# Two-block transformer on one core: values multiplied step by step, latent heads in pairs, side steps one slab later, weight chunks 528 bytes apart

## The reference, cut to what matters

```python
x = first_block(x, c, ctx, c_ctx, ...)    # layer 0: dense GQA + pool mixer; layer 1: window GQA with sink
x = second_block(x, norm_mix_2, ...)      # layer 0: dsa_mixer + diff_mixer; layer 1: nsa_mixer
```

```python
q_lat = einsum('bthd,hdc->bthc', q_nope, w_uk)                 # (T, 8, 128)
s = q_lat . c_kv  +  q_rope . k_rope                           # widths 128 and 32
p = softmax(where(chosen, s * A_SCALE, -inf));  o_lat = p @ c_kv
```

## Time and profile before

| | |
|---|---|
| time, median of 3 runs | 3372.45 us (3364.27 to 3375.6) |
| the profiled execution's own time | 3378.23 us |
| its span | 3376.4 us |
| TensorE busy | 3076.1 us (91%) |
| VectorE, ScalarE, GpSimd busy | 1709.3, 1101.2, 1052.0 us |
| granted TensorE clock, mean | 0.943 |
| matmul records | 16970 |
| HBM read | 253.03 MB, 76 GB/s |

### The profile page before, as it was taken

One profiled execution on the slowest core, in us unless ns is written; L12 is line 12 of the kernel. 1 busy time (PEld: TensorE's weight loads), 2 busy tenths in 40 slices (PEclk: granted clock), 3 DMA queues, 4 the chain that ended last, 5 costly groups with the idle time before them and its releaser, 6 DMA issues.

```text
span 3376.4 us, 48629 instructions
## 1 busy us (share of the span) xinstructions
PE 3076.1 (91%) x16970; PEld 2493.5 (74%) x16970; DVE 1709.3 (51%) x2892; ACT 1101.2 (33%) x1904; POOL 1052.0 (31%) x573
## 2 busy tenths in 40 slices
PE   6778779999997888899998999899999999899997
PEld 3666668888886766699895765688887866688886
DVE  4755768864335566433245766342333247643433
ACT  3145143111124255432224324352223226552222
POOL 1121122323322311244443420244444301244443
PEclk8889989999998899899999988899999969999998
DMA  6200413434211100222222210222223100022222
GB/s 238 77 1 8 142 63 127 171 124 137 75 50 45 43 1 33 67 89 93 94 84 69 75 38 1 80 98 93 93 93 118 55 15 2 14 97 96 93 94 81
DMA packets 74344, 258.83 MB, mean 77 GB/s; under 512 B 9456, under 2 KB 12016, under 8 KB 72688
## 3 DMA queue, kind: packets, MB, share of 16 engines
q1 hardware_dynamic: 60256, 205.61, 18.4%
q10 hardware_dynamic: 13968, 51.65, 4.5%
HBM read 253.03 MB, written 2.10 MB: 76 GB/s over the span
## 4 chain that ended last, share of the span: by engine, by line
PE 81%; DVE 6%; issue 6%; ACT 3%; DVEq 1%; SPq 1%; ACTq 1%; POOL 0%; DMA 0%; POOLq 0%; PEldq 0%
PE ps L822 56%; PE ps L800 6%; PE ps L2513 2%; PE ps L2499 2%; PE ps L2656 1%; PE ps L426 1%; PE ps L1862 1%; PE ps L1095 1%; DVE ps L389 1%; PE ps L2720 1%; PE ps L1666 1%; DVE nm L1711 1%; ACT w_hi L638 1%; PE ps L2633 1%; PE ps L2632 1%
## 5 line engine op out<-in xcount | busy, mean ns | idle before, releaser
L760 POOL TENSOR_TENSOR w_lo<-w_raw,w_hi 128x1024 fp32r<-128x1024 f32 (+1 forms) x373 | 919.6, 2468 | 1823.5 <-ACT w_hi L638 1823.5
L638 ACT ACTIVATE w_hi<-w_raw 128x1024 fp32r<-128x1024 f32 (+1 forms) x373 | 385.6, 1038 | 1192.3 <-PE ps L822 948.0
L822 PE MATMUL ps<-h_hi,w_hi 128*128 128x258 f32 (+2 forms) x1824 | 315.6, 326 | 50.1 <-ACT w_hi L638 46.1
L822 PEld LDWEIGHTS ps<-h_hi,w_hi 128*128 128x128 f32 x1824 | 268.4, 195 | 85.6 <-issue 45.1
L822 PE MATMUL ps<-h_lo,w_hi 128*128 128x258 f32 (+2 forms) x1824 | 299.7, 316 | 0.0
L822 PE MATMUL ps<-h_hi,w_lo 128*128 128x258 f32 (+2 forms) x1824 | 296.7, 314 | 0.0
L822 PEld LDWEIGHTS ps<-h_lo,w_hi 128*128 128x128 f32 x1824 | 260.2, 190 | 24.4 <-DVE h_lo L2275 0.4
L822 PEld LDWEIGHTS ps<-h_hi,w_lo 128*128 128x128 f32 x1824 | 258.4, 189 | 23.1
L918 DVE CAST act_hi<-f_t 128x512 f32 (+1 forms) x88 | 165.8, 1884 | 12.6
L822 PE MATMUL ps<-hb_hi,w_hi 128*128 128x512 f32 x672 | 166.7, 390 | 2.0 <-issue 1.7
L822 PE MATMUL ps<-hb_hi,w_lo 128*128 128x512 f32 x672 | 166.0, 389 | 0.0
(11 more groups left out here) (345 smaller groups left out, 5179.9 us busy)
## 6 DMA issues: line engine op xcount, KB each, us to landing
w_raw<-in_ffn_in SPq DMA_DIRECT2D x176, 512.0 KB, 3.4
mod_row<-in_w_mod_rows ACTq DMA_DIRECT2D x80, 512.0 KB, 4.3
w_raw<-in_ffn_out SPq DMA_DIRECT2D x64, 512.0 KB, 3.4
w_raw<-in_ev_in SPq DMA_DIRECT2D x26, 512.0 KB, 3.5
w_raw<-in_ffn_out SPq DMA_DIRECT2D x32, 384.0 KB, 3.0
w_raw<-in_od_in SPq DMA_DIRECT2D x21, 512.0 KB, 3.4
mod_ring<-in_w_mod SPq DMA_DIRECT2D x8, 1024.0 KB, 13.2
w_raw<-in_wo_in SPq DMA_DIRECT2D x12, 512.0 KB, 3.5
```

Of the source, the lines that this page charges most:

```text
L638: act.activation(k.w_hi[:, s, 0:self.KT * P], k.w_raw[:, s, 0:self.KT * P], ACT.Copy).then_inc(k.sems["w_hi_ready"], 1)
L760: ins = pool.tensor_tensor(k.w_lo[:, s, 0:self.KT * P], k.w_raw[:, s, 0:self.KT * P], k.w_hi[:, s, 0:self.KT * P].bitcast(F32), ALU.subtract)
L822: ins = pe.matmul(k.ps[:, self.step * s + g, 0:t1 - t0], w[:, s, c * P:(c + 1) * P], h[:, c, t0:t1], start=(n == 0), stop=(n == len(parts) ...
```

## The change

1. `PairAttend` gets an option `spread` apart from `one`. The latent stage uses `PairAttend` without either: 4 turns of two heads by 4 query blocks. The value product of a batch takes both heads' probabilities as one moving operand of up to 512 columns. `hn_col` and `hn_rcol` move to make room.
2. `Attend` deals out the products of a batch over the Z steps in every stage, and signals `pv_ready` at i = Z - 1.
3. Side steps 0, 1 and 2 all come after slab 2.
4. In linears with a shift the chunks of `w_hi` and `w_lo` lie 528 bytes apart (`wide = P + 4`); `h_lo` moves by 128 bytes, and the bases of the buffers by multiples of 256.

```diff
+        self.wide = P + (4 if norm is not None and norm.shift is not None else 0)
...
-        act.activation(k.w_hi[:, s, 0:self.KT * P], k.w_raw[:, s, 0:self.KT * P], ACT.Copy).then_inc(k.sems["w_hi_ready"], 1)
+        act.activation(self.parts(k.w_hi, s), self.raw(s), ACT.Copy).then_inc(k.sems["w_hi_ready"], 1)
+    def parts(self, t, s):
+        return t[:, s, 0:self.KT * self.wide].rearrange("p (c w) -> p c w", w=self.wide)[:, :, 0:P]
+    def raw(self, s):
+        return self.kit.w_raw[:, s, 0:self.KT * P].rearrange("p (c w) -> p c w", w=P)
...
-                ins = pe.matmul(..., w[:, s, c * P:(c + 1) * P], h[:, c, t0:t1], ...)
+                ins = pe.matmul(..., w[:, s, c * self.wide:c * self.wide + P], h[:, c, t0:t1], ...)
...
             if self.beside:
-                self.beside.tensor(pe, m)
+                for step in (range(3) if m == 2 else [m]):
+                    self.beside.tensor(pe, step)
...
             self.two(pe, order)
-            if self.beside:
-                for m in range(2):
-                    self.beside.tensor(pe, m)
             self.slabs(pe, tile, 2)
...
-            if self.spread:
-                part = lambda i: len(products) if i else 0
-            else:
-                part = lambda i: len(products) * i // self.Z // 2 * 2 if i < self.Z else len(products)
+            part = lambda i: len(products) * i // self.Z // 2 * 2 if i < self.Z else len(products)
...
-            if i == (0 if self.spread else self.Z - 1):
+            if i == self.Z - 1:
                 ins.then_inc(S["pv_ready"], 1)
...
-            if self.one:
+            if not self.spread:
                 pe.wait_ge(*self.count("prepared", p + 1))
-                if p >= 2:
-                    pe.wait_ge(*self.count("pt_b", p - 1))
+            if self.one and p >= 2:
+                pe.wait_ge(*self.count("pt_b", p - 1))
...
-    k.h_lo = at("h_lo", [P, DC, TOK + 4], F32R, H + 24704)
+    k.h_lo = at("h_lo", [P, DC, TOK + 4], F32R, H + 24832)
-    k.w_hi = at("w_hi", [P, 2, KMAX * P], F32R, W + 8192)
-    k.w_lo = at("w_lo", [P, 2, KMAX * P], F32R, W + 16384)
+    k.w_hi = at("w_hi", [P, 2, KMAX * P + 64], F32R, W + 8192)
+    k.w_lo = at("w_lo", [P, 2, KMAX * P + 64], F32R, W + 16896)
...
+    turns2 = [(j, half) for j in range(2) for half in range(2)]
+    def scores_latent(pe, s, turn, qi):
+        j, half = turns2[turn]
+        n, q = (qi + 1) * P, slice(qi * P, (qi + 1) * P)
+        for a in range(2):
+            pe.matmul(s[:, a, :], k.qlat[:, 4 * j + 2 * half + a, q], k.ckv_s[:, 0:n], start=True, stop=False, skip_group_check=True)
+        for a in range(2):
+            at = 32 * (2 * half + a)
+            rows = slice(at, at + 32)
+            pe.matmul(s[:, a, :], k.qkv2[rows, 12 + j, q], k.qkv2[rows, 1, 0:n], start=False, stop=False, skip_group_check=True, tile_position=(at, 0))
+        for a in range(2):
+            ins = pe.matmul(s[:, a, :], k.ident_b, k.chosen[:, qi, 0:n], start=False, stop=True, skip_group_check=True)
+        return ins
+    def scaled(dve, chain, rinv, probs, turn, qi):
+        return dve.tensor_tensor(probs, probs, rinv.unsqueeze(2).to_broadcast([P, 2, (qi + 1) * P]), ALU.mult)
+    def latent_pv(pe, o, b):
+        both = o.rearrange("p (a q) -> p a q", a=2)
+        for i, (slot, t, c0, c1) in enumerate(causal_terms(b % 2)):
+            ins = pe.matmul(both[:, :, c0:c1], k.ckv_tok[:, t, :], k.pt_pair[:, b % 2, :, slot, c0:c1], start=(i == 0), stop=True, skip_group_check=True)
+        return ins
+    PairAttend(k, len(turns2), scores_latent, latent_pv, scaled, latent_out, k.pt_pair)
```

More of the change, by code:

```diff
@@ L799, in two @@
             for g, (t0, t1) in enumerate(self.groups):
-                ins = pe.matmul(k.ps[:, self.step * s + g, 0:t1 - t0], w[:, s, c * P:(c + 1) * P], h[:, c, t0:t1], start=(e not in begun), stop=(left[e] == 0))
+                ins = pe.matmul(k.ps[:, self.step * s + g, 0:t1 - t0], w[:, s, c * self.wide:c * self.wide + P], h[:, c, t0:t1], start=(e not in begun), stop=(left[e] == 0))
             begun.add(e)
@@ L821, in tile @@
                 for g, (t0, t1) in enumerate(self.columns(m) if self.latent else self.groups):
-                    ins = pe.matmul(k.ps[:, self.step * s + g, 0:t1 - t0], w[:, s, c * P:(c + 1) * P], h[:, c, t0:t1],
+                    ins = pe.matmul(k.ps[:, self.step * s + g, 0:t1 - t0], w[:, s, c * self.wide:c * self.wide + P], h[:, c, t0:t1],
                                     start=(n == 0), stop=(n == len(parts) - 1))
@@ L1802, with __init__ @@
 class PairAttend(Stage):
-    def __init__(self, kit, J, scores, pv, prepare, finish, pt, one, adds=None):
+    def __init__(self, kit, J, scores, pv, prepare, finish, pt, one=False, spread=False, adds=None):
         super().__init__(kit)
+        self.spread = spread
         self.J, self.N, self.B, self.scores, self.pv, self.prepare, self.finish, self.pt, self.one, self.adds = J, J * QT, J * 2, scores, pv, prepare, finish, pt, one, adds
@@ L1816, in __init__ @@
             ("tr_a", 0 if one else self.N), ("pt_a", 0 if one else self.N), ("tr_b", self.N), ("pt_b", self.N),
-            ("pv_ready", self.B), ("spread_ready", 0 if one else self.B), ("o_free", self.B),
+            ("pv_ready", self.B), ("spread_ready", self.B if spread else 0), ("o_free", self.B),
             ("part_ready", self.B if adds else 0), ("part_used", self.B if adds else 0))}
@@ L1868, in output @@
                 pe.wait_ge(*self.count("pt_a", 2 * b + 2))
+            if self.spread:
                 pe.wait_ge(*self.count("prepared", 2 * b + 2))
@@ L1892, in take @@
         def take(b):
-            dve.wait_ge(*self.count("pv_ready" if self.one else "spread_ready", b + 1))
+            dve.wait_ge(*self.count("spread_ready" if self.spread else "pv_ready", b + 1))
             if self.adds and b >= 2:
@@ L1934, in scalar @@
                 exp(p + 1)
-            if not self.one and p >= 3 and p % 2 == 1:
+            if self.spread and p >= 3 and p % 2 == 1:
                 spread((p - 3) // 2)
@@ L1938, in scalar @@
             act.activation(self.turned(p, 0 if self.one else 1), k.ps[:, self.bank(p, 1), 0:(p % QT + 1) * P].rearrange("p (t c) -> p t c", c=P), ACT.Copy).then_inc(S["pt_b"], 1)
-        if not self.one:
+        if self.spread:
             spread(self.B - 1)
@@ L2394, in memory @@
     k.ln_eps = small("ln_eps", [P, 1])
-    k.hn_col, k.hn_rcol = small("hn_col", [P, 64]), small("hn_rcol", [P, 64])
     k.eps = small("eps", [P, 1])
@@ L2628, in plan @@
                  + [{"slab": 14 + m, "hi": k.qkv2_hi[:, 14 + m, :], "lo": k.lo_2[:, m, :]} for m in range(8)], latent_in, d["w_uk"])
-    def scores_latent(pe, s, j, a, qi):
-        rows, n, q = slice(32 * a, 32 * a + 32), (qi + 1) * P, slice(qi * P, (qi + 1) * P)
-        pe.matmul(s[:, 0:n], k.qlat[:, 4 * j + a, q], k.ckv_s[:, 0:n], start=True, stop=False, skip_group_check=True)
-        pe.matmul(s[:, 0:n], k.qkv2[rows, 12 + j, q], k.qkv2[rows, 1, 0:n], start=False, stop=False, skip_group_check=True, tile_position=(32 * a, 0))
-        return pe.matmul(s[:, 0:n], k.ident_b, k.chosen[:, qi, 0:n], start=False, stop=True, skip_group_check=True)
@@ L2636, in whole_pv @@
-    def whole_pv(v, head):
-        def pv(pe, o, j, n):
-            return [lambda i=i, slot=slot, t=t, c0=c0, c1=c1: pe.matmul(
-                o[:, c0:c1], v(j, t), k.pt4[:, n % 2, head(n), slot, c0:c1], start=(i == 0), stop=True, skip_group_check=True)
-                for i, (slot, t, c0, c1) in enumerate(causal_terms(n % 2))]
-        return pv
-    Attend(k, 2, [[(n // 2, 2 * (n % 2) + i, i, True) for i in range(2)] for n in range(8)], scores_latent,
-           causal_tiles, lambda n, qi: 0, whole_pv(lambda j, t: k.ckv_tok[:, t, :], lambda n: n // 2 % 2),
-           lambda dve, chain, j, u, a, qi, probs, rinv: dve.tensor_scalar(probs, probs, rinv, None, ALU.mult), no_marks,
-           lambda dve, chain, o, j, n: dve.tensor_copy(k.qkv2[:, 4 + 4 * j + n // 2, 256 * (n % 2):256 * (n % 2) + 256], o[:, 0:256]), k.pt4)
+    turns2 = [(j, half) for j in range(2) for half in range(2)]
@@ new lines, in scaled, with latent_out @@
+    def scaled(dve, chain, rinv, probs, turn, qi):
[5 more added lines that the diff above has]
+        return ins
+    def latent_out(dve, o, b):
+        first = 4 + 4 * turns2[b // 2][0] + 2 * turns2[b // 2][1]
+        return dve.tensor_copy(k.qkv2[:, first:first + 2, 256 * (b % 2):256 * (b % 2) + 256], o.rearrange("p (a q) -> p a q", a=2))
```

15 lines of the change are left out of this document (5 added, 10 removed).

## The result

The changed kernel takes 3344.65 us (median of 4, 3342.71 to 3347.7) against 3370.89 for the kernel before: ratio 0.9921, interval 0.9907 to 0.9935, so 22 to 31 us less. The forecast was 3357 in a range from 3335. The profiled execution took 3345.04 us, span 3343.3, which is 33.1 less than the profiled one before; that one was some 6 us above the median of its kernel, so differences between these two profiles add up to more than the medians differ by. TensorE is busy 3060.1 us of the span, 92%.

A forecast was written before the change was run, and what follows sets the result against it. TensorE was taken to set the time nearly everywhere, the linears' slabs carrying 56% of the span. Terms -7 (latent pairs), -3 (side steps), 0 (values), -5 (chunks) gave -15 us on the median 3372.45: 3357 us, range 3335 to 3377.

The forecast's parts named there:

- The sum: Whole kernel: -7 - 3 + 0 - 5 = -15 us, on the median 3357 us.
- Latent heads in pairs, -7: Latent stage: one of two rotated products and one switch per block go, one wait is added; -14 to +3 us.
- the wait for `prepared`: Latent stage: TensorE waits before the transposes for VectorE's maximum, copies and scaling, 2.0 us once a turn.
- The VectorE rival: Paired latent stage: scaling late at two blocks a turn, stage keeps 86.6 us, total 3364; chance 0.14 with another rival.
- Values dealt out, 0: Window stages -5 us, dense +3, context +2 from dealing out value products; sum 0, from -8 to +29.
- the price of a switch: Value batches: switching TensorE to two column halves and back takes 0.34 us, paid four times a batch.
- +3 and +2: Dealt-out values: dense stage 3 us longer, context stage 2 us longer.
- The rival of the switches (+29): Value batches: each portion pays 0.34 us and holes stay, +29 us, total 3386; chance 0.12.
- Side steps, -3: `wo_in`: slab 2 starts 2.9 us earlier, nothing gained in `ev_in` and `od_in`; from -4 to +1 us.
- Chunks 528 apart, -5: Shifted linears, 110 slabs: 2 ns a pair saved; bounds a gain of 21 us and a loss of 13.
- the reading of 4 ns between `ha` and `wo_out`: Single 512-column matmuls: part in step 1.98 us, part out of step 2.01, taken as 4 ns a matmul better.
- the distance does nothing: Shifted linears: weights and tokens do not meet in SBUF; weights part 0 to +13 us, total 3366; chance 0.20.

The follow-up runs named there:

- same_32_rows: The changed kernel, but both heads of a pair take their rotated product on the same 32 rows; 0.9940 of the kernel before.
- scale_first: The changed kernel, with VectorE scaling block p+1 before the maximum of block p+2 in all stages with paired heads; 0.9913 of the kernel before.
- values_alone: The kernel before with only the values dealt out over the units; 0.9960 of the kernel before.
- values_in_two: The changed kernel with values of the dense, context and window stages dealt out in two portions a batch instead of four; 0.9961 of the kernel before.
- the second: Profile of `changed_again`, the changed kernel unaltered and measured once more; 3351.28 us, 0.9934 of the kernel before.

## Why the prediction was right, step by step

*The sum* was -15 us and the measurement says -27 and -22. The total lies in the range, and direction and order of size are right. But the largest term was put at nothing (-13.5 measured), and one of -5 and one of -3 do not show in the total; that these errors work against each other is luck. A fifth effect, the clock of the stage behind the latent one, was not in the sum.

*Latent heads in pairs, -7*: right, and so was its working. The turn was put at 17.2 us and is 17.27; the wait for `prepared` at 2.0 us once a turn, and it is 1.79; one rotated product of two gone, by `same_32_rows` 19.20 - 17.27 = 1.93 of the 2.13 (the 128 block's 0.21 fall into the wait, as its expectation had it); the scaling of 768 numbers at 1.0, measured 0.96. The switch is paid once for two heads: the two latent products and then the two rotated ones stand 1.81 and 1.06 us before what follows, 0.10 and 0.21 more than their columns need, as much as one head paid before. The stage is 77.8 instead of 79 to 80, and its time at the lower clock fell from 20.5 to 13.7 us, worth some 3 us at the 0.4 us found above. The VectorE rival (two late blocks, 86.6 us) is out, though `scale_first` shows that its seed was real: 1.6 us a turn were VectorE's order, which I took as given. The whole part measures 11.5 us, 4 more than the stage's forecast.

*Values dealt out, 0*: the term that was mis-sized; alone it measures -13.5 (-9 to -18). For the window batch the step was right in its difference, 0.43 us: its level I read off the shorter of two alternating batches (8.78 in the earlier trace rows; the next before is 9.46). Two batches took 18.24 us, and now the first portions of three batches lie 8.92 + 8.47 = 17.39 apart:

```profile
1176.61 0.44 PE L2508 MATMUL ps<-ident,rinv 128*64 128x128 f32 x4
...
1185.53 0.44 PE L2508 MATMUL ps<-ident,rinv 128*64 128x128 f32 x4
...
1194.00 0.44 PE L2508 MATMUL ps<-ident,rinv 128*64 128x128 f32 x4
```

That is 0.42 a batch. Over the first six batch distances of the two window stages `values_alone` gained 2.9 and 3.0 us, about what the forecast's 0.43 makes of them, and 2.8 more behind the seventh batch's first portion, where each stage ends and where I had expected nothing. In the dense stage the price of a switch was right, 0.36 us measured against 0.34, though one of its pieces was read wrongly (the 0.11 us in the first scores is there without a switch too: 0.57 us from 1213.58 to 1214.15 in the kernel before). What I had too small is what the portions fill: (8.2 - 3) / 8 = 0.65 us a batch in the forecast, 1.08 - 0.09 = 0.99 by the batches' lengths. The holes were there, 7.4 us in the stretch of 69 (the earlier trace rows had said 7 in 85, and I put half of them at the ends), 4.4 of them closed, 0.6 a batch; that the rest was hidden in the tails of the records, as in the window batch of the forecast, is not shown row by row. So the steady batches cost under 0.1 us each, and the end of the stage (22.06 to 20.25 us from the seventh batch's small products to the first of the context stage) and the context stage gave 1.8 and 0.9, where I had +3 and +2. The rival of the switches (+29) is out; `values_in_two` shows that the holes decide more than the switches: it has half of the switches and is 9 to 14 us slower.

*Side steps, -3*: the place was right. In `wo_in` the wait of 6.69 us at line 1095 is gone, and what ends last now is ScalarE's weights of slab 2:

```profile
1066.70 2.61 PE L830 MATMUL ps<-h_hi,w_hi 128*128 128x256 f32 x16 [3.85 <-ACT w_hi L639]
```

6.69 - 3.85 = 2.8 us, put at 2.9. The total of the part alone cannot be told from nothing, nor from -3, and the -4.9 in the first profile was partly the clock's: 136.1 in the second, which is -3.2. The forecast had nothing for `ev_in`, where the late steps cost 0.4 us.

*Chunks 528 apart, -5*: wrong. 349 ns a pair became 350. The step that failed is the reading of 4 ns between `ha` and `wo_out` as an effect of the distance. The difference is still there in the changed kernel (mean distances of starts 227.9 and 230.8 ns), and what makes it stays open. The rival "the distance does nothing" had it, at 0.20. The Trainium skill's rule ("TensorE: Matmul & The Clock Gate", "Step-by-step: what each phase is for") that weight loads take nothing from the running matmul's reads agrees with it: by that rule the term is zero, and it measures 0 us, give or take 3.

*Not in the forecast*: the 6.1 us behind the latent stage, of which 4 belonged to one execution. A forecast made against one profile should have asked how far its clock is its own: before, 41 of that stage's 75 us were at the lower clock, the largest such share of any stage I had windows for.

## What to carry to other kernels

Dealing a burst of TensorE work out over the units that it interrupts is worth it when TensorE has holes inside those units, and it has to be dealt finely enough that no engine behind it goes idle: in the window stretch four portions closed all holes, two hardly any. Each further portion has its price (about 0.36 us here), so it pays only while there are holes to close. When an engine that is late has been idle just before, look at the order of its own queue before counting its work as the price; but that order is right for one stage and wrong for the next, by which of its two products is awaited first. And put the granted clock beside every stage's length before explaining a difference: here equal code differed by 7.6 us in one stage.

## What the runs showed of the hardware

Float32 products on two different 32-row strips start within 10 ns of each other and finish as one (1.13 us for four records of 512 columns, 1.98 on the same strip). Two products on 32 rows cost 0.3 us beyond their columns between products of full height (0.10 before, 0.21 after), as much as one does. One more switch from the full array to column halves and back costs about 0.36 us (dense batches of 9.77 and 10.13 us). The distance of weight chunks, 512 or 528 bytes beside tokens 3088 apart, changes the pace by no more than 1 ns a pair (349.7 to 349.8 against 350.1 to 350.2 ns). The time at the lower clock differs between executions of the same code: six of `scale_first` on one chip had a mean granted clock from 0.946 (3352.49 us) to 0.954 (3336.21 us), and the last attention stage, of one code in 13 profiles, spent 58 us there in 11 of them, 52 in one, and 32 in one, which was 8.6 us shorter for it.
